# The output projection in a decoder step: weights and first tile move into sampled sequence 0, and the channel mixer's states are turned by one transpose

## The reference, cut to what matters

```python
h = rms_norm(x, norm_attn);  proj = h @ w_in          # x_r, q, k, v, gate a, gate b
y_a = rg_lru(causal_dwconv(x_r), ...)                 # and its states
o = attend(q, k, v, lam)                              # differential attention, T5 bias
y_b = rms_norm(o, subln_g) * (1 - lambda_init)
x = x + (g_a * y_a + g_b * y_b) @ w_out               # the output projection
h2 = rms_norm(x, norm_ffn);  up = h2 @ w_up
up_c, new_ffn_buf = causal_dwconv(up, ffn_buf, ...)   # width 3; new_ffn_buf: the last 2 rows
x = x + (gelu(up_c[..., :D_FF]) * up_c[..., D_FF:]) @ w_down
y = rms_norm(x, norm_final)
```

## Time and profile before

| | |
|---|---|
| median of 3 runs | 1960.32 us (1957.76 to 1961.98) |
| profiled execution | 1958.18 us, its span 1956.4 us |
| mean granted TensorE clock | 0.991 of 2.4 GHz |
| TensorE busy | 1894.3 us, 97% |
| VectorE, ScalarE, GpSimd busy | 1277.0, 875.2, 36.4 us |
| DMA | 182.92 MB, mean 93 GB/s |
| stages | heads to 834.2, sampled and out to 1096.8, mixer to the end |

### The profile page before, as it was taken

How to read it: one execution, slowest core, us unless ns; L and a number is a source line. 1 busy time by engine, 2 the same in 40 slices (tenths; PEclk the granted TensorE clock), 3 DMA queues, 4 the chain that set the end, 5 groups by cost and what they waited for, 6 DMA issues and landing times. The chain is left out here.

```text
span 1956.4 us, 37533 instructions
## 1 busy us (share of the span) xinstructions
PE 1894.3 (97%) x13152; PEld 1716.3 (88%) x13152; DVE 1277.0 (65%) x2835; ACT 875.2 (45%) x1693; POOL 36.4 (2%) x68
## 2 busy tenths in 40 slices
PE   6999999999999999859999999999999999999998
PEld 6999999999999999826666998989899999989896
DVE  6766767676767676864544784847576665748476
ACT  6766666665757575742343331313132222314133
POOL 0000000000000000011110000000000000000000
PEclk9999999999999999979999999999999999999999
DMA  6411212121211111298995220202021111202012
GB/s 202 156 56 51 64 48 65 48 65 49 63 51 55 57 53 62 95 385 338 379 343 173 64 65 23 76 8 71 20 66 33 55 44 36 62 23 76 20 37 103
DMA packets 165383, 182.92 MB, mean 93 GB/s; under 512 B 8965, under 2 KB 137509, under 8 KB 165269
## 3 DMA queue, kind: packets, MB, share of 16 engines
q1 hardware_dynamic: 164057, 180.72, 27.9%
q10 hardware_dynamic: 1212, 0.81, 0.1%
HBM read 162.56 MB, written 24.20 MB: 95 GB/s over the span
## 5 line engine op out<-in xcount | busy, mean ns | idle before, releaser
L1275 PE MATMUL ps<-h_hi,w_hi 128*128 128x384 f32 (+1 forms) x1152 | 386.5, 336 | 5.0 <-DVEq L989 3.4
L1275 PE MATMUL ps<-h_hi,w_lo 128*128 128x384 f32 (+1 forms) x1152 | 376.5, 327 | 0.0
L1275 PE MATMUL ps<-h_lo,w_hi 128*128 128x384 f32 (+1 forms) x1152 | 376.4, 327 | 0.0
L2406 PE MATMUL ps<-h_hi,f_w_hi 128*128 128x320 f32 (+1 forms) x1136 | 370.9, 326 | 0.8 <-PEq L1568 0.8
L2406 PE MATMUL ps<-h_hi,f_w_lo 128*128 128x320 f32 (+1 forms) x1136 | 370.5, 326 | 0.0
L2406 PE MATMUL ps<-h_lo,f_w_hi 128*128 128x320 f32 (+1 forms) x1136 | 370.3, 326 | 0.0
L2485 ACT ACTIVATE yc<-ps,f_prm 128x384 f32<-128x384 f32 x144 | 93.4, 653 | 560.8 <-PE ps L2406 396.7
L2386 PE MATMUL ps<-d_hi,act 128*128 128x512 f32 x816 | 257.1, 390 | 0.5 <-issue 0.5
L1275 PEld LDWEIGHTS ps<-h_hi,w_hi 128*128 128x128 f32 x1152 | 217.1, 188 | 9.1 <-issue 4.0
L1275 PEld LDWEIGHTS ps<-h_lo,w_hi 128*128 128x128 f32 x1152 | 217.1, 188 | 0.6
L1275 PEld LDWEIGHTS ps<-h_hi,w_lo 128*128 128x128 f32 x1152 | 216.7, 188 | 0.0
(11 more groups left out here) (306 smaller groups left out, 2900.4 us busy)
## 6 DMA issues: line engine op xcount, KB each, us to landing
k<-in_cache_k SPq DMA_DIRECT2D x64, 512.0 KB, 6.6
vr<-in_cache_v SPq DMA_DIRECT2D x64, 512.0 KB, 6.2
w_raw<-in_w_in SPq DMA_DIRECT2D x48, 512.0 KB, 3.9
f_raw<-in_w_up SPq DMA_DIRECT2D x48, 512.0 KB, 3.8
f_raw<-in_w_down SPq DMA_DIRECT2D x24, 512.0 KB, 3.6
bias<-bias_tiles_dram SPq DMA_DIRECT2D x8, 576.0 KB, 3.7
merged_dram<-mg SPq DMA_DIRECT2D x8, 544.0 KB, 2.7
w_raw<-in_w_out SPq DMA_DIRECT2D x8, 512.0 KB, 8.9
```

Of the source, the lines that this page charges most:

```text
L1275: last_ = pe.matmul(bank(s)[:, 0:n], w[:, W_SLOT[g], k, :], x[:, k, off:off + n], start=(k == 0 and i == 0), stop=(k == KT - 1 and i == 2))
L2406: l_ = pe.matmul(ps[:, e % 6, 0:n], w[:, p, k, :], x[:, k, off:off + n], start=(k == 0 and i == 0), stop=(k == KT - 1 and i == 2))
```

## The change

Four things change.

1. Tile t = b goes with sequence b. Sequence 0 gets all 48 matmuls of tile 0 between `turn_weights(0)` and its first values; `scores(1)` have fills among them as the others; tile 7 goes with sequence 7, and `out_tile` in the tail makes tile 8 alone. `NIN` becomes 8.
2. SP loads w_out (k = 0 first) and the merged tile at the head of the stage, before keys and values; the engines split the weights earlier and in the order 0 to 7. Merged and residual tiles are loaded one sequence sooner. The buffers `P` and `o2s` of the last sequence move to 73728, where tile 7 of `x2` doesn't lie.
3. In the heads' last pass SP takes `("P", GB, 2)` and `STATES_AT` earlier, spreads the loads of sequence 1's keys over later steps, one key page is turned at ("FA",) instead of at the end, and four more query copies are made at ("TW", 7, 1).
4. In the mixer one transpose of 108 columns replaces six of 18, the copy is 128 wide instead of 768, and 12 stores per group replace 4. The load of the mixer's second weight block in the tail waits for `ot_done`.

The tail's order changes with it: `low(0)` before `fold_rows(7)`, `turn(1)` and `turn(2)` directly after the fold, `out_tile(8)` after `turn(5)`, and `residual(8)` after `low(7)`.

```diff
-                for s in (TURN0 if first else TURN):
+                order = TURN0 if first else TURN
+                if last:
+                    order = [x for x in order if x not in (STATES_AT, ("P", GB, 2))]
+                    order[order.index(("P", GB, 1)) + 1:order.index(("P", GB, 1)) + 1] = [("P", GB, 2), STATES_AT]
+                for s in order:
...
-                            if s[1] == GB:
-                                sp.dma_start(c.sbias[:, :], c.sbias_dram.rearrange("a p n -> p (a n)"))\
-                                  .then_inc(c.const_in, 16)
-                                sp.dma_start(c.sel[:, :], ins["pair_select"]).then_inc(c.const_in, 16)
-                                load_next_keys(range(0, 4))
...
+                        if last and s == ("TR", V_, 2):
+                            load_next_keys(range(2, 4))
...
+                        if last:
+                            sp.dma_start(c.sbias[:, :], c.sbias_dram.rearrange("a p n -> p (a n)"))\
+                              .then_inc(c.const_in, 16)
+                            sp.dma_start(c.sel[:, :], ins["pair_select"]).then_inc(c.const_in, 16)
+                            load_next_keys(range(0, 2))
...
-                        spread_queries(act, c, 0, (0, 1))
+                        spread_queries(act, c, 0, (0, 1, 2))
...
-            turn_first(dve, c, c.k_first[6:8])
+            turn_first(dve, c, c.k_first[7:8])
...
-NIN = 7
-KS = (4, 5, 6, 7, 0, 1, 2, 3)
+NIN = 8
+KS = (0, 1, 2, 3, 4, 5, 6, 7)
...
-FIRST_KEYS = {("SB", 5): (0, 1), ("SB", 6): (1, 3), ("SS", 2): (3, 4), ("GAM",): (4, 5), ("FA",): (5, 6)}
+FIRST_KEYS = {("SB", 5): (0, 1), ("SB", 6): (1, 3), ("SS", 2): (3, 4), ("GAM",): (4, 5), ("FA",): (5, 7)}
...
+            merged_low(0)
             new_weights(0)
             for k in POOL_W:
                 weight_low(k)
             for b in range(1, DEC_B):
-                merged_low(b - 1)
+                merged_low(b)
                 new_weights(b)
...
+            def load_weights(ks):
+                for k in ks:
+                    sp.dma_start(w_raw(k), c.w_out[:, k, :]).then_inc(ow_in[k // 2], 16)
+            sp.wait_ge(c.st_out, 64 * (H + 1))
+            load_weights((0, 1))
+            for u in range(2):
+                sp.wait_ge(c.rows_out[u], 64 * (H + 1))
+            load_weights((2, 3))
+            sp.wait_ge(c.whole_sems["mg_out"], 16 * (H + 1))
+            load_m(0)
+            load_weights((4, 5, 6, 7))
+            load_x(0)
+            for n in range(4, NPAGES):
+                load(1, n, ins["cache_k"], k_raw[1][:, n, :], c.k_in[1][n // 2])
             for n in range(NV):
                 load(0, n, ins["cache_v"], vr[:, n, :], c.v_in[n])
-            for n in range(4, NPAGES):
-                load(1, n, ins["cache_k"], k_raw[1][:, n, :], c.k_in[1][n // 2])
-            sp.wait_ge(c.st_out, 64 * (H + 1))
-            for u in range(2):
-                sp.wait_ge(c.rows_out[u], 64 * (H + 1))
-            for k in KS[0:4]:
-                sp.dma_start(w_raw(k), c.w_out[:, k, :]).then_inc(ow_in[1], 16)
-            sp.wait_ge(c.whole_sems["mg_out"], 16 * (H + 1))
-            load_m(0)
             for x in range(2):
                 sp.dma_start(vn_raw[NS * x:NS * (x + 1), :], v_new).then_inc(vn_in, 16)
-            for k in KS[4:8]:
-                sp.dma_start(w_raw(k), c.w_out[:, k, :]).then_inc(ow_in[0], 16)
-            load_x(0)
...
-                if b > 0:
-                    load_m(b)
+                if b < LAST:
+                    load_m(b + 1)
                 load_keys(b + 2, (0, 1))
                 if b > 0:
                     load_values(b, (0, 1))
                     load_values(b, (2, 3))
-                load_keys(b + 2, (2, 3, 4, 5))
-                if 0 < b < LAST:
-                    load_x(b)
+                load_keys(b + 2, (2, 3))
+                if b < LAST - 1:
+                    load_x(b + 1)
+                load_keys(b + 2, (4, 5))
+                if b == LAST - 1:
+                    sp.wait_ge(pt_done, LAST)
+                    load_x(LAST)
                 load_values(b, (4, 5))
                 load_values(b, (6, 7))
                 load_keys(b + 2, (6, 7))
             sp.dma_start(mg[:, :, :], c.merged_dram[:, :, SEQ:NTOK].rearrange("h p n -> p h n")).then_inc(mg_in, 16)
+            sp.wait_ge(ot_done, DEC_B)
             sp.dma_start(c.f_raw[:, 1, :, :], c.w_up[:, :, DFF:DFF + 128]).then_inc(f1_in, 16)
-            sp.wait_ge(ot_done, DEC_B)
-            load_x(NIN)
-            sp.wait_ge(mdlo_done, 2)
+            sp.wait_ge(mdlo_done, 1)
             load_x(NT - 1)
...
             scores(0, {})
             turn_weights(0)
+            fill(0, 2 * HALF)
             values(0, FIRST_HALF)
             for b in range(1, DEC_B):
-                t = b - 1
-                scores(b, AMONG if b > 1 else {})
+                scores(b, AMONG)
                 values(b - 1, SECOND_HALF)
-                fill(t, 8)
+                fill(b, 8)
                 turn_weights(b)
-                if b == 1:
+                if b < LAST:
+                    fill(b, 8)
                     fold_heads(b - 1)
-                    fill(t, 16)
-                    values(b, FIRST_HALF)
-                    fill(t, HALF)
-                elif b < LAST:
-                    fill(t, 8)
-                    fold_heads(b - 1)
-                    fill(t, 16)
+                    fill(b, 16)
                     values(b, FIRST_HALF)
                 else:
-                    fill(t, 4)
+                    fill(b, 4)
                     fold_heads(b - 1)
-                    fill(t, 4)
+                    fill(b, 4)
                     values(b, FIRST_HALF[0:2])
-                    fill(t, 8)
+                    fill(b, 8)
                     values(b, FIRST_HALF[2:4])
-                    fill(t, 8)
+                    fill(b, 8)
                     values(b, SECOND_HALF)
             turn(0)
             fold_heads(LAST)
-            out_tile(NIN, KS[0:4])
+            turn(1)
+            turn(2)
             pe.wait_ge(sq_done, 1)
             pe.matmul(ps[:, 3, :], c.ones[:, :], rs[:, 0, :], start=True, stop=True).then_inc(ss_done, 1)
-            turn(1)
-            out_tile(NIN, KS[4:8])
-            turn(2)
             turn(3)
-            out_tile(NT - 1, KS[0:4])
             turn(4)
-            out_tile(NT - 1, KS[4:8])
             turn(5)
+            out_tile(NT - 1, KS)
             pe.wait_ge(f0_lo, 1)
-            pe.wait_ge(x2_done, 1)
             pe.wait_ge(h2lo_done, 6)
             first_unit(0, range(0, KT))
             turn(6)
...
+            weight_high(0)
+            weight_high(1)
+            merged_high(0)
             copy_weights(0)
-            new_queries(1)
-            for k in KS:
+            for k in range(2, KT):
                 weight_high(k)
-            merged_high(0)
+                if k == 3:
+                    queries(1, (2, 3))
+                    new_queries(1)
             for b in range(1, DEC_B):
-                if b > 1:
-                    merged_high(b - 1)
+                merged_high(b)
...
-            act.wait_ge(m_in, 16 * (NIN + 1))
-            act.wait_ge(half_done, 2 * NIN)
-            act.activation(m_hi[:, :, :], o_raw[:, :, :], ACT.Copy).then_inc(mhi_done, 1)
             copy_o2(LAST)
             high(0)
             act.wait_ge(ots_done, DEC_B)
             act.activation(rs[:, 0, :], oT[:, :, :].rearrange("p h n -> p (h n)"), ACT.Square).then_inc(sq_done, 1)
-            squares(NIN - 1)
+            high(1)
             act.wait_ge(ss_done, 1)
             act.activation(rs[:, 1, :], ps[:, 3, :], ACT.Ln, bias=eps[:, :], scale=1.0 / KV).then_inc(ln_done, 1)
             act.wait_ge(ln_done, 1)
             act.activation(rs[:, 1, :], rs[:, 1, :], ACT.Exp, scale=-0.5).then_inc(rst_done, 1)
-            high(1)
+            high(2)
             act.wait_ge(mgn_done, 1)
-            act.wait_ge(mm_done, 1)
+            act.wait_ge(half_done, 2 * NIN)
             act.activation(m_hi[:, :, 0:NS], mg[:, :, :], ACT.Copy).then_inc(mhi_done, 1)
-            high(2)
             high(3)
-            squares(NIN)
+            squares(NIN - 1)
             high(4)
             high(5)
-            squares(NT - 1)
             high(6)
             high(7)
+            squares(NT - 1)
             high(8)
...
-            turn_keys(1, (4, 5, 6, 7))
             for k in DVE_W:
                 weight_low(k)
+                if k == 3:
+                    turn_keys(1, (4, 5))
+            add_half(0, 0)
+            turn_keys(1, (6, 7))
             for b in range(1, DEC_B):
-                t = b - 1
-                if b > 1:
-                    add_half(t - 1, 1)
+                add_half(b - 1, 1)
                 turn_keys(b + 1, (0, 1))
                 softmax(b)
                 turn_keys(b + 1, (2,))
                 weights(b)
-                if b > 1:
```

(85 more changed lines are left out.)

18 lines of the change are left out of this document (8 added, 10 removed).

## The result

The change makes the kernel slower: median 1969.56 us (1965.44 to 1971.39, 5 runs) against 1958.34 us of the kernel before in the same session, ratio 1.0046 with a 95% interval of 1.0035 to 1.0057. By the ratio that is +9.0 us (+6.9 to +11.2); the two medians of five runs lie 11.2 apart, at the interval's end, so the differences of the experiments are taken from the ratios. I had forecast +3.1, a median of 1963.4. The profiled execution took 1970.62 us, its span 1968.8, which is 12.4 more than before.

What follows compares the result with a forecast made beforehand. TensorE, 97% busy, was taken as the bound except from 834.2 to 898.1. Terms 1.5 - 0.8 + 5.9 - 3.5 = +3.1 gave 1961.3 us profiled, median 1963.4; main case 1958.3 to 1969.7, range 1956.5 to 1970.5.

Steps and rivals of the forecast that it cites:

- Start, -0.3: Heads stage: one key transposition fewer at VectorE's end, against four moved query copies on ScalarE, gives back about 0.3 us.
- Sequence 0's walk: Sequence 0: following the queues from the exponentials' end at 846.45 through weight splits and tile 0, scores(1) start at 877.8.
- 902.4 + 5 x 24.66: Sequences 2 to 7: from scores(2) at 902.4, five steady periods put the last scores at 1025.7, against 1023.91: +1.8 us.
- Loads, -0.8: Last sequence: w_up's load no longer runs beside the last value page, -0.8 us (0 to -1.3); reordered loads charged nothing.
- Tail, +5.9: Tail, from T (first transposes of normalized tile 0) to mixer: +3.7 us at full clock, 2.2 lost clock; +3.7 to +7.1.
- Mixer, -3.5: Mixer: one transpose for six saves 0.55 us in seven groups, less 0.35 for end stores; -4.4 to -2.6.
- the signs that I had named: Included scores(1) near 878, last scores within a few us of 1026, tail near 46 us, clock under 1 in out_tile(8).
- A: Tail: VectorE's chain is covered after all, so faster; 1946 us with W near 0 (0.05), partial cover about 1954 (0.08).
- W: Tail: waits that replace the removed work, counted as 17.2 us (15.0 idle, 2.2 clock); total change is W - 14.1.
- B: Tail: the clock doesn't fall, giving 1961.2 us; chance 0.12.
- C: Sequences 0 to 2 become late through loads or instruction stalls: 1968 us with one, 1972 with two; chance 0.22.
- expected gain of 11.3 us: Tail to sequence 0: 48 matmuls of 512 columns leave the tail for the idle time before 898.1.

Runs made afterwards that it cites:

- experiment 2: Changed kernel with the heads' last pass as it was before (SP's order, keys' turning, query copies): ratio 1.0049 to the kernel before.
- 11: Changed kernel with three squares in place of four on ScalarE at the end of sequence 6: ratio 1.0034 to the kernel before.
- 12: Changed kernel with residual(8), squares(8), norm(3), fold_rows early, w_out 6's low part on VectorE, and three squares in sequence 6: ratio 0.9993 to the kernel before.
- 3: Changed kernel with the sampled tile's residual and squares ahead of low(6) and high(6), norm(8) ahead of low(7): ratio 1.0018 to the kernel before.
- 4: Changed kernel with norm(3) ahead of VectorE's wait for the sampled rows' reciprocal root: ratio 1.0040 to the kernel before.
- 5: Changed kernel with residual(8), squares(8) and norm(3) early and the first up-projection unit ahead of turn(4): ratio 1.0013 to the kernel before.
- 8: Changed kernel with 25 extra matmuls of 512 columns in the tail, 20 ahead of turn(3), 5 ahead of turn(4): ratio 1.0042 to the kernel before.
- 7: Changed kernel with 23 of the 24 matmuls of tile 0's second half left out: ratio 1.0015 to the kernel before.
- 9: Kernel before with the mixer's part, and 24 of tile 0's 48 matmuls moved into sequence 1's page wait: ratio 0.9948, 1949.70 us.
- Kernel 1: Kernel before with the mixer's part of the change alone, without the move of w_up's load: ratio 0.9982 to the kernel before.

## Why the prediction was right or wrong

The sign was right, and so was the account of the tail and of sequence 0: work moved from a place where it hid another engine's chain to one where it costs its time. The size was a third of what was measured. The measured median lies in the range, near its upper end, and in part by luck: two of the four terms, sequence 0's and the loads', lie outside the bounds that I gave them. By terms, from the traces of all kernels that share the code in question:

- **Start, -0.3.** Below the scatter of 2.8 us; experiment 2 finds nothing.
- **Sequence 0's walk, right; what lies around it, mis-sized.** From the end of the exponentials to scores(1) I had 31.35 us; it took 31.9. But seven kernels with this code need 195.4 us on average (193.5 to 197.4) from scores(0) to scores(7), against 189.7 and 189.8 without it: +5.7 in place of +1.8. Two terms failed. The step "902.4 + 5 x 24.66" took the two quietest periods before for all five; the kernel before itself has 125.8 us there, 25.2 each, and these seven average 125.3: 2.0 of it. The other 1.9 lie ahead of scores(2), and 1.3 of them in scores(0), which I had left as before: 9.8 us on average up to its matmuls for the new keys, 8.5 in the kernel before. In the profiled execution it is 2.8: a stall of 2.58 us (1.34 before) and the 109 matmuls behind it at the lower clock (3.92 us, 2.60 before). Of eleven traces with the loads in the new order five have this (11.1 to 11.4 us for scores(0)) and six don't (8.6 to 9.1); the three traces with the old order have 8.8 at most. That w_out's earlier loads make it likelier is not shown.
- **Loads, -0.8.** Wrong in sign: from scores(7) to the tail it is 33.3 us on average in nine traces with this code (32.1 to 34.4), against 32.2 in three without it. The error is a step left out: I followed ScalarE's queue in sequence 0 but not in sequence 6, where a fourth square stands ahead of tile 7's high part. In the changed kernel's trace TensorE waits 1.49 us for it. With three squares (11, 12) both traces have 31.6, which is 0.6 less than without the change and close to the forecast.
- **Tail, +5.9.** Measured +6.0 (46.75 against 40.73), closer than the working deserves. turn(3) came at T + 11.45 (forecast 10.7), turn(5) at 16.8 (16.1), turn(8) at 41.8 (40.6), and from there to the mixer it took 5.0 (3.8). I had put 2.2 us of lost clock into out_tile(8), which runs at the full clock; the loss is in the transposes, where most of it vanishes in waits for VectorE, and in the last twelve matmuls of the up-projection, where it costs 1.2. That the two sums agree is luck. Of my two causes the order of residual(8) is the one that can be mended (3); VectorE's chain stays (4, 5, 8). The Trainium skill, "TensorE: Matmul & The Clock Gate", section on HAM oscillation, says that waits between bursts lower the clock; the 0.73 between 1072.46 and 1084.46 agrees. How much of that reaches the time depends here on whether TensorE is the engine waited for: with the clock kept up in that stretch (8) only 0.6 of the tail went.
- **Mixer, -3.5.** Measured -4.0 in the trace, and -3.5 alone: right.

From the traces 5.7 + 1.1 + 6.0 - 4.0 = +8.8, against the measured +9.0. Two upper bounds were also added up wrongly: sequence 0's parts give +4.7 and not +4.9, the tail's 3.7 + 3.0 = +6.7 and not +7.1. Of the signs that I had named two failed: the last scores came at 1032.1, 6 us after 1026, and out_tile(8) ran at the full clock.

**Rivals:** A is refuted: in the tail W was 46.75 - (40.7 - 11.3) = 17.3, what I had counted. B is refuted, the clock fell. C's time (1968) is near the one measured, and one half of its mechanism came: no page wait appears in sequences 0 to 2, and the stall of 4.6 us that scores(1) had before is in none of the eleven traces with the new order, where fills stand between its matmuls; but scores(0) was late through an instruction stall in five of them. On average that is at most 1.3 of the 5.9 us by which the forecast fell short.

Where the expected gain of 11.3 us went: in the tail, work that covered VectorE's chain was removed (5.9 us of it can be put back at no cost, 8), and in sequence 0 it was put on a chain of splits and ahead of the loads' release, where it costs nearly what it takes (7).

## What to carry to other kernels

An idle stretch is free room only for work on which nothing else waits. Half a tile, some 24 matmuls, cost 6 us ahead of the values on whose slots the loads wait (7). Put into the page wait behind them, in place of a later stretch where TensorE was busy, it saved 7 (9). Before work is taken out of a stretch, ask which chain of another engine it covers: removing it saves nothing below that chain's length. And when a piece of work moves by one step, follow every engine's queue at both ends of the move: one more set of operations of 1.6 us on ScalarE, which is idle for more than half of the time, made TensorE wait 1.49 us.

## What the runs showed of the hardware

- Two executions of the same instructions in scores(0) differ by 2 to 2.8 us: in eight traces a stall of 1.3 to 1.9 us (for nothing that the profile shows) left the clock up and the 109 matmuls behind it took 2.60, in five one of 2.5 to 2.7 us was followed by 3.8 to 3.9. Kernel 1, without a stall there, took 6.75 us for all 256.
- Stalls of over 1 us in the scores came only where the 256 small matmuls stand alone: in scores(0) of thirteen traces, and in scores(1) of the three traces with the old order (4.6 to 5.1 us). With fills between them, the longest in any trace is 0.33 us, at a DMA share of 0.95 to 1.00 in the changed kernel. Whether the fills or something else keep them away no run tells.
- A steady sequence is 24.6 us long in one case and 25.4 in the next, at a clock of 1.00 and with no wait that the profile names: in the changed kernel one group of 64 score matmuls took 1.97 in place of 1.50 us.
